# A conv stage on one core: VectorE's taps placed in the PSUM bank ahead of TensorE's, a two-tap form for two chunks, and four low parts made by VectorE

## What is computed

```python
def conformer_conv(x, w_in, b_in, conv_w, conv_b, ln_g, ln_b, w_out, b_out):
    a, g = jnp.split(x @ w_in + b_in, 2, axis=-1)
    h = a * jax.nn.sigmoid(g)
    # depthwise, causal: 31 taps over the tokens, a weight for each tap and feature
    h = lax.conv_general_dilated(h, conv_w[:, None, :], (1,), [(CONV_KERNEL - 1, 0)],
                                 feature_group_count=D_MODEL) + conv_b
    h = jax.nn.silu(layer_norm(h, ln_g, ln_b))
    return h @ w_out + b_out
```

## Time and profile before

| | us |
|---|---|
| median of 3 runs (lowest to highest) | 1448.66 (1447.51 to 1451.03) |
| the profiled execution, its own time | 1448.54 |
| its span, first to last instruction | 1446.7 |

### The profile page before, as it was taken

One profiled execution on the slowest core, in us unless ns is written; L12 is line 12 of the kernel. 1 busy time (PEld: TensorE's weight loads), 2 busy tenths in 40 slices (PEclk: granted clock), 3 DMA queues, 4 the chain that ended last, 5 costly groups with the idle time before them and its releaser, 6 DMA issues. The chain is left out here.

```text
span 1446.7 us, 19998 instructions
## 1 busy us (share of the span) xinstructions
PE 1429.5 (99%) x6884; PEld 1167.0 (81%) x6884; DVE 923.0 (64%) x1334; ACT 613.0 (42%) x911; POOL 210.0 (15%) x165
## 2 busy tenths in 40 slices
PE   9999999999999999999999999999899999999999
PEld 7788888888887898888888888666588888888887
DVE  7877773573655667767744756899888653544532
ACT  5544442342546665444432424676554322222210
POOL 7100000000302241000000004588411000000000
PEclk9999999999999999999999999999999999999999
DMA  5233233222421012332332322399713332232321
GB/s 191 88 101 102 92 99 114 76 101 89 123 101 59 30 60 88 101 102 87 102 116 73 101 98 91 102 208 233 173 45 102 116 102 89 100 102 87 102 95 51
DMA packets 50140, 148.07 MB, mean 102 GB/s; under 512 B 9376, under 2 KB 10144, under 8 KB 50080
## 3 DMA queue, kind: packets, MB, share of 16 engines
q1 hardware_dynamic: 47216, 138.36, 29.6%
q0 software_dynamic: 2016, 7.34, 2.8%
q10 hardware_dynamic: 848, 1.59, 0.3%
HBM read 137.21 MB, written 2.10 MB: 96 GB/s over the span
## 5 line engine op out<-in xcount | busy, mean ns | idle before, releaser
L610 PE MATMUL bank<-xh,whi 128*128 128x512 f32 x1184 | 465.3, 393 | 0.2
L612 PE MATMUL bank<-xh,wlo 128*128 128x512 f32 x1184 | 461.1, 389 | 0.0
L611 PE MATMUL bank<-xl,whi 128*128 128x512 f32 x1184 | 461.0, 389 | 0.0
L964 ACT ACTIVATE whi<-raw 128x1024 fp32r<-128x1024 f32 x244 | 255.8, 1050 | 254.1 <-PE bank L612 239.4
L1324 DVE TENSOR_TENSOR wlo<-raw,whi 128x1024 fp32r<-128x1024 f32 x230 | 288.7, 1256 | 42.9 <-ACT whi L964 34.8
L610 PEld LDWEIGHTS bank<-xh,whi 128*128 128x128 f32 x1184 | 222.5, 188 | 55.9 <-issue 6.8
L611 PEld LDWEIGHTS bank<-xl,whi 128*128 128x128 f32 x1184 | 222.6, 188 | 46.6 <-issue 1.0
L612 PEld LDWEIGHTS bank<-xh,wlo 128*128 128x128 f32 x1184 | 222.4, 188 | 46.3
L610 PE MATMUL bank<-ahi,whi 128*128 128x512 f32 x608 | 236.5, 389 | 0.0
L611 PE MATMUL bank<-alo,whi 128*128 128x512 f32 x608 | 236.5, 389 | 0.0
L612 PE MATMUL bank<-ahi,wlo 128*128 128x512 f32 x608 | 236.5, 389 | 0.0
(11 more groups left out here) (187 smaller groups left out, 1308.2 us busy)
## 6 DMA issues: line engine op xcount, KB each, us to landing
raw<-w_ffn_up SPq DMA_DIRECT2D x88, 512.0 KB, 3.3
raw<-w_ffn_down SPq DMA_DIRECT2D x32, 512.0 KB, 3.2
raw<-w_mlp_up SPq DMA_DIRECT2D x32, 512.0 KB, 3.2
raw<-w_mlp_down SPq DMA_DIRECT2D x32, 512.0 KB, 3.3
raw<-w_ain SPq DMA_DIRECT2D x16, 512.0 KB, 4.9
raw<-w_ffn_down SPq DMA_DIRECT2D x16, 384.0 KB, 3.0
raw<-w_qkv SPq DMA_DIRECT2D x12, 512.0 KB, 3.4
shifted<-hc SPq DMA_DIRECT2D x20, 258.0 KB, 5.8
```

The source lines that it names most:

```text
L610: nc.tensor.matmul(out_, hi, mh, start=first, stop=False)
L611: nc.tensor.matmul(out_, hi, ml, start=False, stop=False)
L612: return nc.tensor.matmul(out_, lo, mh, start=False, stop=last)
L964: nc.scalar.activation(whi[:, s, 0:tiles * P], raw[:, s, 0:tiles * P], ACT.Copy)\
```

## The change

1. **Shares of the taps** (`PE_TAPS`, `SHIFTS`, `POOL_TAPS`, `LATE_TAPS`). By chunk 0 to 7, before and after:

| | before | after |
|---|---|---|
| TensorE | 8 8 8 8 8 12 20 14 | 6 6 8 8 12 12 20 14 |
| shifts | 4 4 4 4 4 4 4 2 | 2 2 4 4 4 4 4 2 |
| products | 10 9 9 8 8 8 7 6 | 11 10 10 9 9 9 8 6 |
| own | 11 10 8 6 3 2 4 11 | 12 7 3 2 1 3 3 11 |
| late | 2 4 6 9 12 9 0 0 | 2 8 10 12 9 7 0 0 |

2. **Own taps go into the bank of the taps**, except in chunk 7 (`APART`). TensorE waits for them in front of its taps and adds to what lies there (`start` is false). `collect` has one add less in seven chunks. Two matmuls in `first_chains` write banks 6 and 7 once, so that later matmuls add.
3. **Units 6 to 9 get their low part from VectorE** (`split_lo`), not from an adding transfer. The adding transfers of units 17 to 19 are all issued after GpSimd's last add, and ScalarE splits and negates these units in chunk 7.
4. **Order of VectorE near the end**: the diagonals and the gating of chunk 7 come before `collect(5)`.

```diff
-PE_TAPS = (8, 8, 8, 8, 8, 12, 20, 14)
-SHIFTS = (4, 4, 4, 4, 4, 4, 4, 2)
+PE_TAPS = (6, 6, 8, 8, 12, 12, 20, 14)
+SHIFTS = (2, 2, 4, 4, 4, 4, 4, 2)
+APART = C - 1
-POOL_TAPS = (10, 9, 9, 8, 8, 8, 7, 6)
-LATE_TAPS = (2, 4, 6, 9, 12, 9, 0, 0)
+POOL_TAPS = (11, 10, 10, 9, 9, 9, 8, 6)
+LATE_TAPS = (2, 8, 10, 12, 9, 7, 0, 0)
-LOW_AT = {6: (0, 7), 7: (0, 9), 8: (1, 5), 9: (1, 7), 10: (2, 5), 11: (2, 7), 12: (3, 5), 13: (3, 7), 14: (4, 5),
-          15: (4, 7), 16: (5, 6), 17: (6, 5), 18: (7, 1), 19: (7, 5)}
+LOW_AT = {10: (2, 5), 11: (2, 7), 12: (3, 5), 13: (3, 7), 14: (4, 5), 15: (4, 7), 16: (5, 6), 17: (7, 5), 18: (7, 5),
+          19: (7, 5)}
...
+                    if name == "ain" and t == 0:
+                        for b in range(2):
+                            nc.tensor.matmul(bank[6 + b][:], whi[:, 0, 0:P], xh[:, 0, :], start=True, stop=True)
...
                 if c >= 2:
                     pe.wait_ge(hv_ready, c - 1)
+                if c != APART:
+                    pe.wait_ge(tap_steps, sum(len(own_taps(e)) for e in range(c + 1)))
                 for q in range(ROUNDS[c]):
...
-                                              start=(q == 0), stop=(q == ROUNDS[c] - 1))
+                                              start=(q == 0 and c == APART), stop=(q == ROUNDS[c] - 1),
+                                              skip_group_check=True)
...
-                        negate_high(e)
+                        if e in ADDED:
+                            negate_high(e)
...
-                for e in {C - 2: (17, 18), C - 1: (19,)}.get(c, ()):
+                for e in (17, 18, 19) if c == C - 1 else ():
                     split_hi(p.unit, 0, e)
                     negate_high(e)
...
                 x, w = hc[:, c % HC, k:k + T], v("conv_w", c * TAPS + k)
+                at = taps[:] if c == APART else bank[6 + c % 2][:]
                 if n == 0:
-                    V.tensor_scalar(taps[:], x, w, None, ALU.mult).then_inc(tap_steps, 1)
+                    if 2 <= c != APART:
+                        dve.wait_ge(hv_ready, c - 1)
+                    V.tensor_scalar(at, x, w, None, ALU.mult).then_inc(tap_steps, 1)
...
-                if own_taps(c):
+                if c == APART:
                     dve.wait_ge(tap_steps, sum(len(own_taps(j)) for j in range(c + 1)))
                     V.tensor_tensor(hv[:, c, :], part, hv[:, c, :], ALU.add).then_inc(own_added, 1)
...
-                if j and c:
-                    dve.wait_ge(tap_steps, sum(len(own_taps(e)) for e in range(c)))
...
-                diagonals(c)
+                if c < C - 1:
+                    diagonals(c)
...
+                if c == C - 2:
+                    diagonals(C - 1)
+                    gated(C - 1)
                 if c:
                     collect(c - 1)
-                if c == C - 2:
-                    gated(C - 1)
```

More of the change, by code:

```diff
@@ L334, in build, with own_taps @@
         dist = cst[:, CST_DIST:CST_DIST + 2 * P]
+        def own_taps(c):
+            return range(PE_TAPS[c] + POOL_TAPS[c], TAPS - LATE_TAPS[c])
         def o_at(t, s):
@@ L1667, in _ @@
             V.memset(hc[:, :, 0:TAPS - 1], 0.0).then_inc(hc_ready, 1)
-            def own_taps(c):
-                return range(PE_TAPS[c] + POOL_TAPS[c], TAPS - LATE_TAPS[c])
             def late_taps(c):
@@ L1677, in own_tap @@
                 x, w = hc[:, c % HC, k:k + T], v("conv_w", c * TAPS + k)
+                at = taps[:] if c == APART else bank[6 + c % 2][:]
                 if n == 0:
-                    V.tensor_scalar(taps[:], x, w, None, ALU.mult).then_inc(tap_steps, 1)
+                    if 2 <= c != APART:
+                        dve.wait_ge(hv_ready, c - 1)
+                    V.tensor_scalar(at, x, w, None, ALU.mult).then_inc(tap_steps, 1)
                     return
                 dve.wait_ge(tap_steps, sum(len(own_taps(j)) for j in range(c)) + n)
-                V.scalar_tensor_tensor(hv[:, c, :] if n == len(own_taps(c)) - 1 else taps[:], x, w, taps[:],
+                V.scalar_tensor_tensor(hv[:, c, :] if c == APART and n == len(own_taps(c)) - 1 else at, x, w, at,
                                        op0=ALU.mult, op1=ALU.add).then_inc(tap_steps, 1)
@@ L1715, in collect @@
                     part = hv[:, c, :]
-                    dve.wait_ge(own_added, sum(1 for j in range(c + 1) if own_taps(j)))
+                    dve.wait_ge(own_added, 1)
                 dve.wait_ge(late_steps, sum(LATE_TAPS[:c + 1]))
```

## The result

| | before | after |
|---|---|---|
| median of 20 runs each, same chip (lowest to highest) | 1449.86 (1447.51 to 1452.46) | 1451.92 (1449.81 to 1454.12) |
| the profiled execution, its own time | 1448.54 | 1453.63 |
| its span | 1446.7 | 1451.9 |

The ratio after to before is 1.0015, with a 95% interval of 1.0009 to 1.0022: the change makes the kernel 2.2 us slower (1.3 to 3.2), inside the 0.3% that was called no change. The forecast was +2.5 us. So the total came out, and the question of the study is whether its four terms did. They did not all: in the profiled execution two were off by over a microsecond, in opposite directions.

What follows compares the result with a forecast made beforehand. TensorE was taken as the bound, with holes only in the conv stage. The terms, 0.3 + 0.86 + 1.6 - 0.3 = +2.5 us on the profiled 1448.54, gave 1451.0 us, range 1446.5 to 1455.5.

Steps and rivals of the forecast that it cites:

- Term 1: Chunks 0 and 1, two-tap form: gain at chunk 1 spent on chunk 0's wait for own taps; +0.3 us (-0.4 to +1.5).
- Term 2: Chunk 4: 12 taps for 8 on TensorE, 24 records for 16; +0.86 us.
- Term 3: Chunks 3 and 4: VectorE, with new low parts, issues the copies late and TensorE waits; +1.6 us (-0.6 to +5).
- Term 4: End of conv stage: chunk 7's eviction goes 0.3 us earlier, hole 2.6 becomes 2.3; -0.3 us (to -2.0).
- Work at no price: Conv stage: ScalarE's seven more products, GpSimd's seven more adds and late transfers of units 17 to 19 cost nothing.
- rival (d): First output units: low parts 17 and 18 late, 2 us and slow start of 1.7 on top, 1454.7; chance 0.04.
- (a): Conv stage: VectorE becomes the bound, over 3 us wait and half clock at chunk 4; +5.9, 1454.4 us; chance 0.24.
- (b): Conv stage: copies stop mattering, no waits at chunks 3 and 4, last hole at full clock; -1.4, 1447.1; chance 0.16.
- (c): Chunk 0: own taps end when the copies did, 936.6, so 3.8 us less; with (b) 1443.3; chance 0.06.

Runs made afterwards that it cites:

- The first experiment: The changed kernel with the low parts of units 6 to 9 made by adding transfers again, not by VectorE; 1450.54 us, ratio to before 1.0009.
- two-way kernel: The kernel before with the new end of the stage and 12 of chunk 0's taps on TensorE, two shifted copies for chunk 0; 1448.69 us, ratio 0.9994.
- 12 taps four-way: The kernel before with the new end of the stage and 12 of chunk 0's taps on TensorE, four shifted copies; 1448.18 us, ratio 0.9980.
- third experiment: The changed kernel with all own taps in their own bank again, no priming matmuls; 1453.47 us, ratio to before 1.0023.

## Why the prediction came out, point by point

**Term 1, chunks 0 and 1: right in its mechanism and nearly in size.** Predicted: a hole of 5.7 us, 2.6 + 1.7 us of taps, nothing at chunk 1, in total +0.3. Shown: 5.95 us for VectorE's taps, 4.43 us for the 12 records, no hole at chunk 1. To the start of taps 2, a point that holds the whole of the exchange, the difference is 0.24 us, and with the priming matmuls +0.70. The 0.4 too little: 0.25 of hole, and a chunk 1 whose taps take 2.8 where 2.6 was set (12 records are six passes and 0.2 to drain, as the prediction had itself read at chunk 7). Its own steps end at 958.4 against 958.19, which is +0.2 and not +0.3. The chain of waits was right, VectorE's own taps decide and not the copies: with chunk 0 apart the hole is gone.

**Term 2, chunk 4: right.** 24 records take 2.78 us for 1.93, and the step to taps 5 is +0.88 against +0.86 forecast.

**Term 3, the low parts: right cause, size too small, and one part of it hit by luck.** Forecast +1.6; shown +1.88 and +1.06 at chunks 3 and 4, in total +2.9. The holes were set at 0.5 and 1.7; they are 1.80 and 1.65. VectorE was late as counted: 2.2 us behind TensorE at the eviction of chunk 3 (975.01 against 972.8; forecast 2.0) and 2.1 at that of chunk 4 (988.27 against 986.2; forecast 2.7). The low part itself was a little oversized, 1.84 for a mean of 1.70 of the four new ones (1.60, 1.67, 2.29, 1.22; unit 5's, at 946.71, was VectorE's before too). The step that failed is the last one, from VectorE's lateness to the hole. At chunk 3 the prediction let 1.5 us of 2.0 disappear without a row. At chunk 4 it had the copies there 8.0 to 12.4 us after their issue; it took 13.4, from 989.83 to the taps at 1003.26. That its 1.7 us met the measured 1.65 is luck: it is the middle between no wait and the longest, while the middle of its landing times (997.6) less TensorE's arrival (996.4 to 997) gives 0.6 to 1.2, and the copies were issued less late and took longer than it had them. SP's issues of the four copies of chunk 4 of after, and the medians from issue to landing for those of chunks 3 and 4:

```profile
989.83 7.05 SPq L488 DMA_DIRECT2D shifted<-hc  x4
```

```profile
shifted<-hc SPq DMA_DIRECT2D x4, 258.0 KB, 7.6
...
shifted<-hc SPq DMA_DIRECT2D x4, 260.0 KB, 8.4
```

The four issues of chunk 4 took SP 7.05 us where they took 4.34 in before, and a copy 8.4 us to land where it took 6.3; at chunk 3 it was 7.6 and 7.5. Copies issued later were no faster, so most of the lateness came through to TensorE: 3.45 us of 4.3 at the two chunks. How it falls on them differs by execution: VectorE 1.9 and 1.8 us late gave holes of 0.89 and 2.19 (old order), 2.7 and 2.6 us late gave 2.01 and 0.83 (transfers early). Against before's 0.58 the three executions make term 3 2.9, 2.5 and 2.3 us, the last with 1.0 us of slow start besides. The first experiment shows the cause: without the four low parts VectorE waits for TensorE again and the holes are 0.53 and 0.91.

**Term 4, the end of the stage: right sign, wrong cause, size too small.** Forecast -0.3 from the order of VectorE's work, down to -2.0 without a slow start. Shown: the hole 1.68 for 2.60, the 28 records 6.23 for 7.93, in total -2.6, of which 0.4 was given back (below). The order gives nothing: undone, it changes nothing. The copies do go out 0.3 us earlier in after, 1.68 us behind the start of chunk 6's taps for 1.98, as forecast; but they do so in the old order too, because VectorE no longer comes late to the eviction. The rest comes from the adding transfers of units 17 and 18, which used to be under way when chunk 7's copies were; without them the copies land 0.9 to 1.1 us earlier, and the shorter hole has no slow start. This is what the traces show of chunk 7; in the runs the late transfers were worth 0.6, 0.9 and 1.3 us (before with the new end, the early transfers, before with the late transfers alone), none of them clear of noise. The prediction saw that these transfers move and asked only whether they would be in time for their own use. It did not ask what they had been beside. That is the step that failed.

**Work at no price: one item had one.** ScalarE's six passes for units 17 to 19 were to end at 1038, 3.6 us behind the start of chunk 7's taps by the forecast's own shift (1034.4); they end at 1043.97, 5.6 us behind it. A table load follows, and only then the squares of chunk 7 (line 1264). TensorE waits 0.96 us for them, for 0.64 in before, and from the sums' side the whole end is 0.4 us later than the taps of chunk 7 make it. The transfers of units 17 to 19 were issued up to 1045.1, and the output projection began without a wait for them: rival (d) did not come. GpSimd's seven more adds cost TensorE nothing, but they are what the low parts stand beside.

**The rivals.** (a) VectorE as the bound was to bring over 3 us and a slow start at chunk 4; it was 1.65 us and full clock. Its direction was right. By the Trainium skill (GPSIMD Engine Reference, Specifications) GpSimd's SBUF interfaces are shared with VectorE, with contention for VectorE instructions that have two SBUF inputs. The trace agrees on average and not for each instruction: the low part took 1.22 us in the quiet stretch and 1.70 on average of the four new ones, but one at 936.30, with GpSimd adding all the while (934.96 to 944.30), took 1.22 as well, and the same one 2.21 in the kernel with eight own taps. (b) had two halves: the slow start at chunk 7 did go, the waits at chunks 3 and 4 did not. (c) did not come: the own taps of chunk 0 end 6.2 us into the scale (943.40), and 6.05 was counted.

In this pair of profiles terms 1 and 3 and ScalarE were too small by 0.4, 1.3 and 0.4 us, term 4 by 2.3 us the other way: together 0.2. That the sum was met this closely is chance; two misses of over a microsecond cancelled, and what the working had earned was the range.

## What to carry to other kernels

When a transfer is moved, ask what it ran beside and not only whether it is in time where it now is: two entries of a table took the long hole and the slow start at chunk 7 away. When an engine that feeds copies becomes late by some microseconds, carry the lateness through to the reader of the copies unless a row shows copies that got faster; here half to four fifths of it arrived. And where several engines run with nearly the same beat, price a part by taking it out alone: here a hole of 6 us was worth 2, as the next waits stood right behind it.

## What the runs showed of the hardware

The cost of a hole at the clock is not fixed by its length. The same wait of 5.94 or 5.95 us in front of chunk 0's 12 records was in four kernels; from those taps to chunk 1's it took 15.47 us (after), 15.71 (old order), 16.25 (low parts back) and 16.69 (transfers early), and in after from chunk 1's to chunk 2's, with the same matmuls, 13.84. So the slow start cost 1.6, 1.9, 2.4 and 2.8 us. Behind the holes of 1.15 to 1.96 us at chunk 7 there was no loss in any of twelve kernels. With holes of 2.0 to 2.4 us both occurred: before's 2.31 was followed by slow taps (2.67 us for 16 records), and so was the two-way kernel's 2.13 (2.83 for 16, above); the kernel with the new end alone, which has before's instructions up to there, had 2.37 and full speed:

```profile
937.62 1.92 PE L883 MATMUL bank<-shifted,dg 128*32 128x512 f32 x16 [2.37 <-DMA shifted<-hc]
```

The half clock can also come where no such hole stands, as in the layer norm above. Three of the fourteen profiles have it there (eight own taps, 2.4 us; late transfers alone, 2.4; 12 taps four-way, 0.8), behind waits of 0.3 to 1.0 us. All three are among the twelve with late transfers, but nine others of these do not have it, and only two profiles have the transfers early, so whether the late transfers bring it on, and take back part of their gain, is open. The layer norm, chunk 1's four copies, whose hole was 3.42, 5.26 and 4.65 us in three kernels with the same instructions up to there, the slow starts above, and the start of the first projection (28.86 to 31.59) are the differences found that could put executions of one kernel 6 us apart. They are read from single profiles and not counted, and the 3.9 us between profile and median of the third experiment stay open.

Of VectorE's work the making of the diagonals showed the largest factor beside GpSimd: one of the same form, 128x384, took 0.56 us in iteration 0, before GpSimd's first add, and 1.72 in iteration 4, beside its adds (at 932.00 and 989.84 of after).
